# A two-block transformer kernel: twenty modulation steps go ahead of the small vectors, the lambda and rotation tables move into the first projection, and the scale's first columns get a PSUM bank of their own

## The reference

```python
mod = silu(c) @ w_ada + b_ada              # 2048 x 12288: six vectors of 2048 (N_MOD = 6)
shift, scale = mod[0:2048], mod[2048:4096] # of the mixing half; four more groups follow later
h = rmsnorm(x, g_norm_mix) * (1 + scale) + shift
proj = h @ w_in                            # 256 x 2048 by 2048 x 3904
# proj holds q, k, v of a differential attention and the latents of an MLA attention;
# cos/sin of positions * theta turn part of q and k;
lam = exp(lambda_q1 . lambda_k1) - exp(lambda_q2 . lambda_k2) + lambda_init
```

## Time and profile before

| | us |
|---|---|
| median of 3 runs | 2860.73 (2860.21 to 2864.05) |
| the profiled execution, own time | 2855.52 |
| its span | 2853.8 |
| PE busy | 2654.4 (93%) |
| DVE busy | 1655.3 (58%) |
| ACT busy | 1198.4 (42%) |

### The profile page before, as it was taken

How to read it: one execution, slowest core, us unless ns; L and a number is a source line. 1 busy time by engine, 2 the same in 40 slices (tenths; PEclk the granted TensorE clock), 3 DMA queues, 4 the chain that set the end, 5 groups by cost and what they waited for, 6 DMA issues and landing times.

```text
span 2853.8 us, 31351 instructions
## 1 busy us (share of the span) xinstructions
PE 2654.4 (93%) x12111; PEld 2184.9 (77%) x12111; DVE 1655.3 (58%) x1800; ACT 1198.4 (42%) x1574; POOL 9.5 (0%) x62
## 2 busy tenths in 40 slices
PE   0499678899999999999999989999999999999999
PEld 0388556778888888888888866888888888888887
DVE  6767778667645555556655736454555545445554
ACT  1243334344443444444444634444454434344443
POOL 0000000000000000000000000000000000000000
PEclk9999789999999999999999969999999999999999
DMA  8887466757755556555554521556556565555554
GB/s 338 303 275 272 153 221 238 255 202 280 247 193 195 188 181 203 192 191 181 192 174 159 169 74 59 192 181 202 179 174 207 177 202 180 201 187 191 187 192 147
DMA packets 254800, 565.99 MB, mean 198 GB/s; under 512 B 9959, under 2 KB 25060, under 8 KB 242148
## 3 DMA queue, kind: packets, MB, share of 16 engines
q1 hardware_dynamic: 252164, 562.87, 58.3%
q10 hardware_dynamic: 2530, 1.65, 0.2%
HBM read 562.39 MB, written 2.10 MB: 198 GB/s over the span
## 4 chain that ended last, share of the span: by engine, by line
PE 88%; DVE 8%; issue 1%; DMA 1%; ACT 1%; ACTq 1%; DVEq 0%
PE acc L414 81%; DVE acc_ada L1372 3%; PE tp L428 3%; DVE w_lo L367 1%; PE acc L2651 1%; PE acc L2722 0%; DMA perow<-in_cmp_pe_v_dram 0%; PE acc L2721 0%; PE tp L2301 0%; ACTq L640 0%; DVE mxs L1616 0%; PE sc L2706 0%; PE sc L2704 0%; ACT w_hi L362 0%; DMA w_raw<-in_w_ada_dram 0%
## 5 line engine op out<-in xcount | busy, mean ns | idle before, releaser
L367 DVE TENSOR_TENSOR w_lo<-w_raw,w_hi 128x1024 fp32r<-128x1024 f32 (+3 forms) x882 | 1054.8, 1217 | 597.6 <-ACT w_hi L362 591.5
L362 ACT ACTIVATE w_hi<-w_raw 128x1024 fp32r<-128x1024 f32 (+3 forms) x882 | 915.8, 1056 | 878.1 <-PE acc L414 828.4
L414 PE MATMUL acc<-w_hi,h_hi 128*128 128x512 f32 (+2 forms) x2272 | 705.8, 392 | 15.9 <-DVE h_lo L1443 11.1
L414 PE MATMUL acc<-w_hi,h_lo 128*128 128x512 f32 (+2 forms) x2272 | 699.3, 389 | 0.0
L414 PE MATMUL acc<-w_lo,h_hi 128*128 128x512 f32 (+2 forms) x2272 | 699.1, 389 | 0.0
L414 PEld LDWEIGHTS acc<-w_hi,h_hi 128*128 128x128 f32 x2272 | 421.6, 189 | 100.4 <-DVE h_lo L1443 12.4
L414 PEld LDWEIGHTS acc<-w_hi,h_lo 128*128 128x128 f32 x2272 | 427.5, 188 | 87.7
L414 PEld LDWEIGHTS acc<-w_lo,h_hi 128*128 128x128 f32 x2272 | 427.5, 188 | 87.6
L414 PE MATMUL acc<-w_hi,f_hi 128*128 128x512 f32 x864 | 268.5, 392 | 0.0
L414 PE MATMUL acc<-w_hi,f_lo 128*128 128x512 f32 x864 | 266.2, 389 | 0.0
L414 PE MATMUL acc<-w_lo,f_hi 128*128 128x512 f32 x864 | 266.2, 389 | 0.0
(11 more groups left out here) (392 smaller groups left out, 1722.0 us busy)
## 6 DMA issues: line engine op xcount, KB each, us to landing
w_raw<-in_w_ff_dram SPq DMA_DIRECT2D x128, 1024.0 KB, 5.4
w_raw<-in_w_in_dram SPq DMA_DIRECT2D x108, 1024.0 KB, 5.0
w_raw<-in_w_ada_dram SPq DMA_DIRECT2D x96, 1024.0 KB, 5.1
w_raw<-in_w_ffn_gate_dram SPq DMA_DIRECT2D x44, 1024.0 KB, 5.1
w_raw<-in_w_ffn_up_dram SPq DMA_DIRECT2D x44, 1024.0 KB, 5.0
w_raw<-in_w_ffn_down_dram SPq DMA_DIRECT2D x44, 1024.0 KB, 5.0
w_raw<-in_w_out_dram SPq DMA_DIRECT2D x32, 1024.0 KB, 5.0
w_raw<-in_w_up_fox_dram SPq DMA_DIRECT2D x8, 1024.0 KB, 5.1
```

The costliest lines, as they stand in the source:

```text
L362: nc.scalar.activation(dst, src, ACT.Copy).then_inc(hi_done, 1)
L367: nc.vector.tensor_tensor(dst, src, hi.bitcast(F32), ALU.subtract).then_inc(lo_done, 1)
L414: last = nc.tensor.matmul(acc[b][:, t, 0:width], st[:, kt, t * P:(t + 1) * P], w[:, slot, kt - 2 * j, 0:width], start=(kt == 0 and n == 0) ...
```

## The change

DVE runs 20 modulation steps before anything else, copies the gains (`vecB`), and has the norm of x and the shift column between steps 21 and 24; nothing of the front waits on DVE for `small_loaded` any more (PE's transpose of rowsB does). The lambda dots, positions, angles and lambda operations move into chunks 1, 4 and 5 of the projection, at fixed halves, and so do ACT's exponential (chunk 1) and sines (chunk 5). So that these chunks exist one by one in the lists of ACT and DVE, their loop covers chunks 2 and 3 only (`uniform=4` for 6). The scale's 16 column sums go into `sc`, four columns into `sc[0]` and twelve into `sc[1]`, with a signal after each, behind the transposes of pieces 0 and 1 in PE's list. Scale and `gmod` are made in two parts, and pieces 0 and 1 come behind halves 0 and 1. `mod_made` counts one more. The pieces now take the uses 3 to 10 of `tp`.

```diff
@@ ACT
-            act.wait_ge(S("lambda_dots"), 1)
-            nc.scalar.activation(lamb[:, 2:4], lamb[:, 0:2], ACT.Exp).then_inc(S("lambda_exp"), 1)
-
-            act.wait_ge(S("angles_reduced"), 1)
-            nc.scalar.activation(cosm[:], angr[:, 0, :, 0:32], ACT.Sin)
...
+            def lambda_exp(j):
+
+                if j == 5:
+                    act.wait_ge(S("lambda_dots"), 1)
+                    nc.scalar.activation(lamb[:, 2:4], lamb[:, 0:2], ACT.Exp).then_inc(S("lambda_exp"), 1)
+
+            def rope_tables(j):
+
+                if j == 7:
+                    act.wait_ge(S("angles_reduced"), 1)
+                    nc.scalar.activation(cosm[:], angr[:, 0, :, 0:32], ACT.Sin)
...
+            def first_mix(j):
+
+                if j < 2:
+                    if j == 0:
+                        act.wait_ge(S("mod_made"), 1)
+                    mix_piece(j)
+                elif j > 3:
+                    if j == 4:
+                        act.wait_ge(S("mod_made"), 2)
+                    mix_piece(j - 2)
+                    if j == KD // 2 - 1:
+                        mix_piece(j - 1)
+                        mix_piece(j)
+
+            weights(8, KD, copy_out(proj, KD, w7), uniform=4, widths=w7, macs=2, first=first_mix,
+                    during={1: lambda_exp, 5: rope_tables})
@@ DVE
-            macs(8)
-            dve.wait_ge(S("small_loaded"), 16 * SMALL)
...
+            macs(20)
+            bank, free = tp_wait(dve, At(1))
+            V.tensor_copy(vecB[:, 0:NROWS], bank[:, 0:NROWS]).then_inc(free, 1)
             macs(2)
+            norm("mix")
+            macs(1)
+            scaled("mix", range(2, 4))
+            macs(1)
+            mod_column(0, 2)
+            macs(2 * KD - macs_so_far)
+
+            def first_scales(ks, bank):
+
+                link(V.tensor_tensor(modT[:, KD + ks.start:KD + ks.stop], bank[:, ks], vecA[:, KD + ks.start:KD + ks.stop],
+                                     ALU.add))
+                link(V.scalar_tensor_tensor(gmod[:, ks], modT[:, KD + ks.start:KD + ks.stop], 1.0,
+                                            vecA[:, 112 + ks.start:112 + ks.stop], ALU.add, ALU.mult))
+                dve.sem_inc(S("mod_made"), 1)
+
+            dve.wait_ge(S("scale_sums"), 1)
+            first_scales(slice(0, 4), sc[0])
...
+            def first_mix(j):
+
+                if j < 2:
+                    mix_piece(j)
+                    if j == 1:
+                        dve.wait_ge(S("scale_sums"), 2)
+                        first_scales(slice(4, KD), sc[1])
...
+            weights(8, KD, copy_out(proj, KD, w7), uniform=4, widths=w7, macs=2, first=first_mix,
+                    during={1: lambdas, 4: positions, 5: other_angles, 6: rope_early})
@@ PE
             ada_sum(0, 2)
-            ada_sum(1, 3)
+
+            def scale_sums():
+
+                pe.wait_ge(S("mac_done"), 2 * KD)
+                for k in range(KD):
+                    last = MM(sc[k >= 4][:, k:k + 1], acc_ada[1][:, k * P:(k + 1) * P], ones[:, 0:1], start=True, stop=True)
+                    if k in (3, KD - 1):
+                        last.then_inc(S("scale_sums"), 1)
...
                         for p in range(2):
                             turn(p)
+                        if tag == "mix":
+                            scale_sums()
```

More of the change, by code:

```diff
@@ L769, in _ @@
             n.load = 2 * KD
-            use = 4
+            use = 3
             w7 = {7: IN1 - 7 * CW}
-            weights(8, KD, copy_out(proj, KD, w7), uniform=6, widths=w7, macs=2,
-                    first=first_chunk(lambda: act.wait_ge(S("mod_made"), 1),
-                                      modulated("mix", use, gmod[:, 0:KD], modT[:, 0:KD])))
+            mix_piece = modulated("mix", use, gmod[:, 0:KD], modT[:, 0:KD])
+            def first_mix(j):
[12 more added lines that the diff above has]
+                    during={1: lambda_exp, 5: rope_tables})
             use += 8 + 1
@@ L911, in _ @@
                 weights(8, KD, relu_drain, late=f_hi_out, macs=0 if part else 2, leave_last=True, first=first_chunk(
-                    lambda: (act.wait_ge(S("mod_made"), 2), norm("ff")),
+                    lambda: (act.wait_ge(S("mod_made"), 3), norm("ff")),
                     modulated("ff", use, gmod[:, KD:2 * KD], modT[:, 3 * KD:4 * KD]),
@@ L1409, in _, with angles @@
+            def angles(q):
+                turn = (0.25, 0.0)[q]
                 link(V.tensor_scalar(angk[:, q], ang[:, 1], float(1 / (2 * np.pi)), turn, ALU.mult, ALU.add))
@@ L1417, in _, with positions, other_angles @@
                 link(V.tensor_scalar(angr[:, q], angr[:, q], PI_IN, -PI_IN, ALU.min, ALU.max))
[L1418 to L1438, removed]
+            def positions(j):
+                if j == 3:
+                    link(V.tensor_copy(pos_f[:], pos_i[:]))
+                    dve.wait_ge(S("inv_made"), 1)
+                    for t in range(NT):
+                        link(V.tensor_scalar(ang[:, 1, t, :], inv[:], pos_f[:, t:t + 1], None, ALU.mult))
+                elif j == 5:
+                    angles(0)
+            def other_angles(j):
+                if j == 4:
+                    angles(1)
+                    dve.sem_inc(S("angles_reduced"), 1)
             def split_sbuf(src, hi, lo, done):
@@ L1561, in _ @@
             w7 = {7: IN1 - 7 * CW}
-            use = 4
-            weights(8, KD, copy_out(proj, KD, w7), uniform=6, widths=w7, macs=2, during={6: rope_early},
-                    first=first_chunk(lambda: None, modulated("mix", use)))
+            use = 3
+            mix_piece = modulated("mix", use)
+            def first_mix(j):
[4 more added lines that the diff above has]
+                        first_scales(slice(4, KD), sc[1])
+                elif j > 3:
+                    mix_piece(j - 2)
+                    if j == KD // 2 - 1:
+                        mix_piece(j - 1)
+                        mix_piece(j)
+            weights(8, KD, copy_out(proj, KD, w7), uniform=4, widths=w7, macs=2, first=first_mix,
+                    during={1: lambdas, 4: positions, 5: other_angles, 6: rope_early})
             all_drained("proj_made")
@@ L2373, in _ @@
             w7 = {7: IN1 - 7 * CW}
-            weights(8, KD, h_hi, h_lo, uniform=6, widths=w7, first=modulated("mix", 4))
-            use = 12
+            weights(8, KD, h_hi, h_lo, uniform=6, widths=w7, first=modulated("mix", 3))
+            use = 11
             ada_sum(2, use)
```

34 lines of the change are left out of this document (20 added, 14 removed).

## The result

The changed kernel takes 2842.5 us, the median of four runs (2840.19 to 2843.58), against 2860.47 of the kernel before (four runs): ratio 0.9934, 95% interval 0.9917 to 0.9952, 18.0 us faster. The forecast was 2841.7 in a range of 2836 to 2850.

The account below looks back on a forecast made before the run. The prediction took PE's matmul stream to bound nearly all of the kernel, so an earlier projection start would pay: 11.4 us ahead of T plus 7.6 behind it, 19.0 off 2860.7, giving 2841.7 us, range 2836 to 2850.

Parts of the forecast that it names:

- T: End of modulation step 31 in the front: 107.4 before, forecast 96.0, a gain of 11.4 us, bounds 7.9 and 14.3.
- the doubtful 2.70: Microseconds per load if loads 13 to 31 go half at 2.53 and half at 2.87, giving T 96.4.
- the 2.5 us behind step 21: Front: norm and four scaled pieces on DVE after step 21, 2.5 us, during which loads land ahead.
- Behind T: From T to the first projection matmul: 14.7 us before, 7.1 forecast with PE's sums ending last, a gain of 7.6 us.
- M - T: Time from T to M, the start of the first projection matmul: 14.7 us before, forecast 7.1, M near 103.1.
- The pattern of chunk 0: First projection chunk: runs in its old pattern, with its wait of 1.90 us before half 3.
- The moved work costs nothing: Small operations moved into the projection cost 0: largest block 1.9 us, DVE 5.6 us ahead of PE.
- (a): Rival: transfers bound the front, loads 2.8 us or slower, T 99.5 to 103.9, time 2845 to 2850; chance 0.12.
- (b): Rival: PE reaches its higher clock earlier, half 0 takes 2.7 us less (under 4), time 2837 to 2839; chance 0.12.
- (c): Rival: moved blocks starve PE in the projection, 3.6 us each; chance 0.02 of loss over 0.2%, 0.04 of breaks within it.
- (d): Rival: the front is not the bound, its gain is lost in a later wait, time 2860; chance 0.02.

Follow-up runs that it names:

- only the wait moved: Kernel before, with the wait for the small vectors and the lambda, position and angle work moved from behind step 7 to behind step 19: 2854.43 us, ratio 0.9974.
- the tail undone: Changed kernel with all 16 scale sums under one signal ahead of the transposes, and pieces 0 and 1 behind half 3 again: 2852.58 us, ratio 0.9961.
- the warm start: Changed kernel plus nine unused 128x512 matmuls on PE, spread over modulation steps 26 to 31: 2839.19 us, ratio 0.9915.
- the block five times as long: Changed kernel with the first block of angles run five times in a row in chunk 4 of the projection: 2851.07 us, ratio 0.9957.
- in the repeat: Under (a), the kernel with nine extra PE matmuls ahead of the column sums, run again without further edit: 2843.80 us, ratio 0.9934.
- both repeats: The changed kernel run two more times without any edit: 2845.19 us (ratio 0.9932) and 2841.87 us (ratio 0.9942).
- The repeat's chain: Chain from the first unedited rerun of the changed kernel: 2845.19 us, ratio 0.9932 to the kernel before.
- the exchange: Changed kernel with DVE splitting its activation piece before the modulation step in chunk 0's halves: 2844.42 us alone, 2840.96 with the warm start.

## Why the prediction was right

**T.** Said 96.0, measured 95.52, 95.26 and 95.51: a term of 11.9 for 11.4. Loads of steps 4 to 17 came 2.57 us apart ((56.02 - 22.65) / 13), between the 2.53 taken and the doubtful 2.70. The load pace ended there and not at step 21, as was said. Of the 2.5 us behind step 21 all is there as well, and 0.65 us more behind the shift column, a wait that wasn't seen coming and whose cause no row shows. The kernel with only the wait moved splits this term in two (6.0 and 5.9), and the one with the tail undone keeps all of it (T 95.47).

**Behind T.** Said 7.1, measured 6.90; a term of 7.85 for 7.6. The first split stands at T + 4.7 (said 4.9), so the sums end last, as forecast, 2.2 us behind the split (102.42 - 100.26). With the sums halved by the warm start, M - T falls to 3.99, and then PE waits 0.20 us for the split, which has become the later of the two.

**The pattern of chunk 0** stayed: 1.94 us before half 3, behind the modulation step that DVE does first (1.90 before).

**The moved work costs nothing.** PE has no idle from half 4 to the end of the projection, and the block five times as long, 10.0 us, cost 5.0 of idle, against a lead of 5.6 read from the earlier trace rows.

**The rivals.** (a), loads of 2.8 us: not over the whole front in any execution; but in the two profiles of the warm start the loads of steps 4 to 21 came 2.67 and 2.71 us apart, the last four of them 2.8 in the repeat, and T was 97.6 and 98.3, so the worry was right in kind and half its size. (b), the clock: half 0 took 4.34 and in both repeats 5.10 to 5.12, before 5.49, never under the 4 that would have shown (b). Coming straight from the sums doesn't settle it: half 0 took 4.22 to 5.33 in the seven profiles in which it does, and 5.49 three times and 4.70 once where PE had been idle. With the half behind the wait (3.02, but 4.61 in the repeats) the clock gave 2.5 us in the first execution and almost nothing in the others. The repeat's chain:
```profile
102.30 5.10 PE acc L414 x12
...
116.36 4.61 PE acc L414 x12
```
(c) didn't come. (d) can't be told from scatter: in the profiled executions the three stages in which PE stops and goes took 2 to 10 us longer than before, by the clock, and no run shows that the change is the cause.

**The sum.** 19.0 was said, 19.7 to 20.4 came at M, 17.2 to 18.1 in the medians of the three comparisons. What was too simple is to count every us gained at the projection's start as gained at the end: the three later stages differ by 3.6 us among three executions of the changed kernel alone and by 4.0 between two of before, and whether 1 or 2 us of the gain are lost there stays open. That 0.8 us separates the forecast of 2841.7 from the median is partly luck, since the median itself moved by 3 us from one comparison to the next. What the runs bear out is the mechanism and the sizes of the two terms when both are changed.

## What to carry to other kernels

A wait in a loop fed by loads costs less than it shows, because the loads catch up in it: the wait of 9.0 us was worth 6.0, since without it the steps up to 17 wait for their loads. The 6.2 us of small work, taken out where DVE sets the pace, was worth 5.9. Work on PE that doesn't need the last input should be done before it comes, so that only the reductions stand between it and the first matmul; they need banks that are free by then, and can be handed over in parts. Small work is free inside a stream of matmuls as long as its largest block stays under the consumer's lead, here some 5 us.

## What the runs showed of the hardware

- TensorE's level in stages with many short stops is a matter of the execution: the same 323 matmuls in 97.3, 100.4 or 103.0 us at 0.95, 0.90 and 0.87. Half 3 behind a stop of 1.9 us ran in 3.02 or 4.61 in one and the same kernel.
- One-column sums don't bring the higher level by themselves (6.99 us of them, and half 0 still starts at 0.43 us a matmul), but use it where they find it (3.73). They don't hold it either: behind 7.54 us of the added matmuls without a break (88.39 to 95.93) and 3.72 of sums, with the warm start and the exchange, half 0 took 4.35 us and most of it ran at the lower level, the granted clock at 0.52 from 101.6 to 103 us. In both 6.99 and 3.73 the granted clock read 1.00, so here it's the durations that tell the level.
- Loads of 1 MB, queue kept full: 2.43 to 2.71 us each, 401 to 424 GB/s, a difference that moved T by up to 3 us. The slow pace was seen in the two profiles of one kernel only; whether it belongs to that kernel or to the execution isn't shown.
- GpSimd and DVE: a 128x2048 tensor-scalar took 2.85 us beside a GpSimd clearing of 1.80, 1.28 alone. Two-input splits beside the same clearing kept their pace (2.36 for two). The Trainium skill (GPSIMD Engine Reference, Specifications) has the two engines contend when DVE is in a two-port mode or has two inputs from SBUF; the first agrees with these rows, though none of them names the mode; the second doesn't show in them, but the clearing reads nothing, so they don't test two readers.
